# Low parts of normed and convolved tiles move from GpSimd to VectorE

## The reference

```python
proj = _rms(x, g) @ w_in                    # one projection for both branches
u = conv_in[..., :D_CONV] * sigmoid(conv_in[..., D_CONV:])        # GLU columns
c = conv(u_pad, w_dw) + b_dw                # causal depthwise, 31 taps
conv_out = silu(_layernorm(c, ln_conv_g, ln_conv_b)) @ w_o_conv
pr = proj[..., OFF_RWKV:OFF_GATE]           # RWKV-7 columns, token shift
pm = pr + (pr_prev - pr) * mu_shift
```

## Time and profile before

| | before |
|---|---|
| timed runs | 1696.54, 1700.61, 1701.82 us (median 1700.61) |
| profiled execution | 1696.31 us, span of the trace 1694.6 us |
| TensorE busy | 1535.2 us, 91% of the span; mean granted clock 0.939 |
| VectorE, ScalarE, GpSimd busy | 844.9, 478.2, 560.9 us |
| low parts of weights on GpSimd | 149 instructions, 375.2 us |
| glu slots | to about 88 us |
| rkv and lora slots | about 88 to 280 us |
| gate slots | about 280 to 396 us |
| conv slots | 402 to 443 us |

### The profile page before, as it was taken

The page is one execution under the profiler, slowest core; times in us unless marked ns, Lnnn a source line. Parts: engine busy times, 40 slices in busy tenths (PEclk is TensorE's granted clock), DMA queues, the critical chain, the costliest instruction groups (busy, mean ns, idle before and its releaser), DMA issues.

```text
span 1694.6 us, 34717 instructions
## 1 busy us (share of the span) xinstructions
PE 1535.2 (91%) x14036; PEld 1425.6 (84%) x14036; DVE 844.9 (50%) x1172; ACT 478.2 (28%) x735; POOL 560.9 (33%) x340
## 2 busy tenths in 40 slices
PE   6999999998875899988979999869999999999995
PEld 5899999997523799974779899529999999999995
DVE  5489999704497666347426750335522112211246
ACT  4222222224551232412222342422333212211221
POOL 3655552035361000001444113005544334433441
PEclk9999999999866899987799999889999999999997
DMA  4122235223300111213131352361222222222222
GB/s 151 63 74 74 74 81 82 74 104 109 113 0 9 17 15 16 62 60 145 38 149 63 125 173 74 155 261 62 75 74 74 75 75 74 74 74 75 74 80 81
DMA packets 75847, 141.00 MB, mean 83 GB/s; under 512 B 43328, under 2 KB 46016, under 8 KB 73712
## 3 DMA queue, kind: packets, MB, share of 16 engines
q1 hardware_dynamic: 71760, 134.30, 24.8%
q0 software_dynamic: 1280, 5.24, 0.8%
q10 hardware_dynamic: 2720, 0.20, 0.1%
HBM read 124.76 MB, written 12.99 MB: 81 GB/s over the span
## 4 chain that ended last, share of the span: by engine, by line
PE 30%; issue 18%; POOL 9%; DVE 6%; ACT 2%; DMA 1%; SPq 1%; POOLq 0%; DVEq 0%; ACTq 0%; PEldq 0%
PE ps L393 16%; PE ps L498 9%; POOL wlo L371 7%; POOL hdl L1881 2%; PE ps L2064 1%; DMA kc<-in_kc 1%; DVE ar L1633 1%; PE ps L1991 1%; PE ps L2073 1%; PE ps L1942 1%; DVE wlo L341 1%; ACT pex L1351 0%; ACT whi L335 0%; PE ps L434 0%; DVE ht L1775 0%
## 5 line engine op out<-in xcount | busy, mean ns | idle before, releaser
L371 POOL TENSOR_TENSOR wlo<-raw,whi 128x1024 fp32r<-128x1024 f32 x149 | 375.2, 2518 | 535.5 <-ACT whi L360 535.2
L360 ACT ACTIVATE whi<-raw 128x1024 fp32r<-128x1024 f32 x158 | 166.8, 1055 | 288.4 <-PE ps L393 277.7
L393 PE MATMUL ps<-fnl,whi 128*128 128x320 f32 x704 | 160.8, 309 | 0.0
L393 PE MATMUL ps<-fnh,whi 128*128 128x320 f32 x704 | 160.4, 309 | 0.0
L393 PE MATMUL ps<-fnh,wlo 128*128 128x320 f32 x704 | 160.3, 309 | 0.0
L393 PE MATMUL ps<-xnl,whi 128*128 128x320 f32 x672 | 153.8, 310 | 2.9 <-POOL wlo L371 1.5
L393 PE MATMUL ps<-xnh,wlo 128*128 128x320 f32 x672 | 153.2, 309 | 0.0
L393 PE MATMUL ps<-xnh,whi 128*128 128x320 f32 x672 | 153.0, 309 | 0.0
L393 PEld LDWEIGHTS ps<-fnl,whi 128*128 128x128 f32 x704 | 117.7, 188 | 0.3
L393 PEld LDWEIGHTS ps<-fnh,whi 128*128 128x128 f32 x704 | 117.8, 188 | 0.0
L393 PEld LDWEIGHTS ps<-fnh,wlo 128*128 128x128 f32 x704 | 117.7, 188 | 0.0
(11 more groups left out here) (334 smaller groups left out, 3331.7 us busy)
## 6 DMA issues: line engine op xcount, KB each, us to landing
raw<-in_slots SPq DMA_DIRECT2D x174, 512.0 KB, 3.3
kc<-in_kc SPq DMA_DIRECT2D x4, 2048.0 KB, 8.9
vc<-in_vc SPq DMA_DIRECT2D x8, 1024.0 KB, 8.4
xin<-in_x SPq DMA_DIRECT2D x4, 640.0 KB, 7.8
tmp_g<-tmp POOLq DMA_DIRECT2D x8, 320.0 KB, 2.5
tmp_m<-pr POOLq DMA_DIRECT2D x8, 320.0 KB, 3.6
m1t<-tmp_m SPq DMA_DIRECT2D x1, 2560.0 KB, 12.7
t2t<-tmp_g SPq DMA_DIRECT2D x1, 2560.0 KB, 18.6
```

Source lines behind the costliest of these rows:

```text
L360: nc.scalar.activation(whi[s][:].rearrange("p a b -> p (a b)"), raw[s][:], ACT.Copy).then_inc(S["w_hi"], 1)
L371: on.tensor_tensor(wlo[s][:].rearrange("p a b -> p (a b)"), raw[s][:], whi[s][:].rearrange("p a b -> p (a b)").bitcast(F32), ALU.subtract) ...
L393: last = nc.tensor.matmul(cut(ps[s], h, n), a[:, k, :], b[:, k, h * w:(h + 1) * w], start=(k == 0 and q == 0), stop=(k == k_tiles - 1 and ...
```

## The change

GpSimd no longer makes the low parts of the eight normed tiles and of the four convolved tiles; VectorE does. In the glu slots VectorE does two of them at the end of each pair, behind the GLU product. In the conv stage it does tile j-1 behind the product of tile j, and the last one at the end. The work itself, its order in the tiles and all other instructions stay.

```diff
 (VectorE, glu slots, end of pair i)
+                for k in (2 * i, 2 * i + 1):
+                    dve.wait_ge(S["xh_ready"], k + 1)
+                    nc.vector.tensor_tensor(xnl[:, k, :], xnf[k % 2][:], xnh[:, k, :].bitcast(F32), ALU.subtract).then_inc(S["xl_ready"], 1)
                 dve.wait_ge(S["u_ready"], i + 2)
                 dve.wait_ge(S["ug_ready"], 3 * i + 3)
             dve.sem_inc(S["pr_free"], 2)
 (VectorE, conv)
+            def conv_low(j):
+                dve.wait_ge(S["ch_ready"], j + 1)
+                nc.vector.tensor_tensor(cl[:, j, :], acc[:, j, :], ch[:, j, :].bitcast(F32), ALU.subtract).then_inc(S["cl_ready"], 1)
+
             for j in range(CT):
                 dve.wait_ge(S["ct_ready"], j + 1)
                 nc.vector.scalar_tensor_tensor(out=acc[:, j, :], in0=up[:, j, 0:NT], scalar=1.0, in1=acc[:, j, :],
                                                op0=ALU.add, op1=ALU.mult).then_inc(S["cs_ready"], 1)
+                if j:
+                    conv_low(j - 1)
+            conv_low(CT - 1)
 (GpSimd, glu slots)
                 lo_part(pool, i, 2)
-                for k in (2 * i, 2 * i + 1):
-                    low_tile(pool, 0, k, k % 2, xnh, xnl, n_bufs)
 (GpSimd, conv)
-            for j in range(CT):
-                await_(pool, S["ch_ready"], j + 1)
-                nc.gpsimd.tensor_tensor(cl[:, j, :], acc[:, j, :], ch[:, j, :].bitcast(F32), ALU.subtract).then_inc(S["cl_ready"], 1)
```

## The result

The changed kernel's median is 1690.32 us (1688.23 to 1693.05, 5 runs), that of the kernel before 1699.05 us beside it (1696.54 to 1701.82, 5 runs). The ratio is 0.9951, with a 95% interval of 0.9935 to 0.9967: 8.3 us less, between 5.6 and 11.0. Ten further runs of the same kernel on another occasion gave 0.9962 (0.9946 to 0.9977), 6.5 us less. I had forecast 1692.5 us, 6.1 less, in a range from 1688 to 1699.

The account below looks back on a forecast made before the run. TensorE, busy 91% of the span, bounds the kernel, so only its waits can be won: 3.5 (glu) + 1.2 (slot 9) + 1.4 (conv) = 6.1 us, from 1698.6 to 1692.5 us, range 1688 to 1699.

Parts of the forecast that it names:

- The four waits of the glu stage: TensorE's waits for GpSimd's weights at slots 3, 5, 7 (3.80 us) and 9 (1.51); first three to save 3.5.
- The collision: Glu slots: VectorE's second subtraction and GpSimd's weights' low part become ready together, one waits; 0.1 us left per pair.
- The 2.5 us that I named as a possible sign: Glu slots: each second new VectorE subtraction would take near 2.5 us where GpSimd went first.
- Rival B: Glu turns harm GpSimd: 1.0 of each 1.27 us wait stays, 0.8 at slot 9; saves 2.9, 1695.7 us; chance 0.18.
- The cover on VectorE: Glu slots: VectorE's two subtractions, 1.66 us per pair, hide in a hole of more than 2 before L1438.
- Slot 9: End of the glu stage: of TensorE's 1.51 us wait 0.3 stays, 1.2 saved.
- Does it last: Slot 9 to conv: VectorE's backlog grows about 1.3 us, is caught up in nine slots; the whole 4.7 carries over.
- C: Glu win given back before the recurrence, first gate slot waits longer; only 1.4 us saved, 1697.2 us; chance 0.1.
- D: VectorE becomes the bound in the 26 shift slots; at 0.6 us more per slot, net 5.6 slower, 1704.2; chance 0.05.
- Conv: Conv start after 4.9 us instead of 6.0; second slot's weights earlier, TensorE waits about 0.9 for them; 1.4 us saved.
- the bound of 0.9: First conv slot: a later clock rise loses 0.9 us hidden by the wait for weights; 0.9 more kept as bound.
- The clock: Conv slots: TensorE restarts at half clock; a shorter gap wins nothing, a later rise may lose 0.9 us.

Follow-up runs that it names:

- the order experiment: Kernel before, no work moved: in the glu slots GpSimd makes the odd slot's weights' low part before the two normed tiles; ratio 0.9971.
- doubled work: Changed kernel with each of VectorE's eight glu subtractions done twice, the first into a scratch tile; slots 8 and 9 lose 1.87 us in all.
- all together: Changed kernel, ScalarE's conv tanh and rounding interleaved, six normed tiles back on GpSimd behind odd slots' weights, merged tiles' low parts on VectorE; 0.9942 of before, 1688.38 us.

## Why the prediction was right, point by point

**The four waits of the glu stage.** Right in place and mechanism. "3.80 - 0.3 = 3.5" was too small: slot 7 is done 4.24 us earlier. The 0.1 left per pair is what the trace shows (14.19 against 14.08). The term mis-sized is the wait itself, taken at its listed 1.27; by the order experiment it cost 1.52, so three of them 0.74 more than the sum had.

**The collision.** Right that it comes in the second subtraction and that GpSimd waits for one instruction only; VectorE was first in all four pairs, and its eight subtractions take 0.82 each. The 2.5 us that I named as a possible sign did not appear. Rival B is out: even doubled work brought no wait in slots 3 to 7.

**The cover on VectorE.** 2.68 us of idle time before L1438, 1.55 us of work. Right; doubling it cost nothing until slot 9.

**Slot 9.** 1.2 forecast, 1.74 measured (5.98 at slot 9 less 4.24 at slot 7). I had allowed for the increment to pass the running subtraction; it passed two. The 0.54 more are the 0.3 that I had kept as a remainder, and again the 0.25 by which a wait costs more than it lists.

**Does it last.** Right. VectorE's starts of L1503 come 6.76 to 7.01 us apart up to 169 us and 7.04 after that, TensorE's own pace, so it has caught up. The first gate slot waits 1.3 as before; rivals C and D are out. 0.27 us are given back in one gate slot, which the prediction had not. There GpSimd issues its first DMA 3.7 us after ScalarE's tanh, where before it took 1.6, and the slot behind starts with a 0.56 pair. The issue is late (3.6 to 3.9) in all seven traces in which VectorE makes the eight low parts, with 0.1 to 0.4 us lost by the last gate slot, and on time with nothing lost in the six others, "all together" with two of the eight on VectorE among them. So it goes with the glu edit. The profile names no wait for it, and why it is late stays open; nothing was tried on it.

**Conv.** 1.4 forecast, 1.61 measured, start after 4.87 us (4.9 forecast), low parts at the times given within 0.2. The second slot's weights come 1.6 us earlier than before, counted from the last gate slot, and the head sum does too. That they alone decide holds for the second trace, where TensorE waits 0.78 for them (0.9 forecast). In the first, at half clock throughout the slot, TensorE came only as they did. That both traces end with the same 1.6 is in so far luck; had the clock risen later still, some of it would have gone, as the bound of 0.9 allowed.

**The clock.** I had kept only 0.9 us for it and looked only at the conv slots. The part behind the head sum, the same code, took 1266.6 to 1271.6 us in ten traces, and in the one stage followed up (the 32 matmuls above) the granted clock went with the 1.7 us between them. That scatter is more than what lies between 7.3 and the 8.7 by which the two medians differ, and it is not the change's. Which execution gets which clock, and what makes up the rest of the 5 us, stays open.

**The sum.** 6.1 forecast; 7.3 at the head sum by the traces, 6.5 to 8.3 by the ratios. 6.1 + 0.74 (three waits) + 0.54 (slot 9) + 0.21 (conv) - 0.27 (gate slot) = 7.3: one of the errors went the other way. The absolute time, 1692.5 forecast and 1690.3 measured, is no finer a test than that, since the medians of one kernel move by more than 2 us between occasions (1690.3 and 1692.9 for the changed kernel).

## What to carry to other kernels

Before work is moved to another engine, look at the order on the engine that is late: here a third option, the same work one place later in GpSimd's program, brought 0.29% of the 0.4 to 0.5% and left VectorE alone. Price a wait of TensorE at its listed length plus what the list leaves out (0.25 us here). When an instruction is moved ahead of another, ask what both engines hold at that moment: an earlier low part on GpSimd cost VectorE's chain 2.2 us and the kernel more than the wait it removed. And before a fraction of a microsecond is put down to an edit next to a change of the clock, see how long the clock was low in each trace.

## What the runs showed of the hardware

- A wait of TensorE costs more than the trace lists: 1.27 us listed, 1.52 by the length of the pair: the list starts at the recorded end of a matmul (0.31 us), where the next could have started after 0.147, and the first matmul behind the wait holds the next for 0.25. An operand that arrives in the last instant costs 0.1 without any wait being listed.
- VectorE with two SBUF inputs and GpSimd take turns by whole instructions. GpSimd's 2.41 us became 2.91 behind a started 0.82, VectorE's 0.82 became 3.00 and 3.03 behind GpSimd. The Trainium skill, SBUF — State Buffer, "Who interferes with whom", says that the second to issue blocks until the first is through; both rows agree. That VectorE gets no two turns in a row while GpSimd waits, the doubled run shows; that GpSimd gets none either, the rows of before: VectorE's L1451 (43.73, 1.67 long) ended at 45.40, between GpSimd's two low parts (43.37 to 46.84).
- An increment of a semaphore on VectorE went out while two subtractions ahead of it had not ended (GpSimd's copy, which the profile puts down to it, starts at 87.34, they end at 88.49).
- The same 32 matmuls took 9.2 or 10.9 us in different executions of one kernel, with a granted clock of 1.00 or 0.87 in the window around them.
- After the idle time ahead of the first conv slot TensorE ran at half clock for 6.2 us in one trace of the changed kernel and 4.0 in the other; in before it was 3.7.
